# Eight terms of a depthwise convolution, for two of four channel tiles, as diagonal products on TensorE

## The reference, cut to what matters

```python
def conformer(glu):
    val, gate = jnp.split(glu, 2, axis=-1)
    y = depthwise_conv(val * jax.nn.sigmoid(gate), dw_conv) + dw_bias
    return jax.nn.silu(layer_norm(y, cln_g, cln_b))

def merge(o, z, glu):
    o = rms_norm(o, out_norm) * jax.nn.silu(z)
    return jnp.concatenate([o.reshape(B, L, GDN_WIDTH), conformer(glu)], axis=-1) @ w_out
```

## Time and profile before

| | |
|---|---|
| median of 3 runs | 2729.27 us |
| the profiled execution | 2721.98 us, span 2720.2 us, mean granted TensorE clock 0.978 |
| TensorE busy | 2588.2 us (95%) |
| VectorE busy | 1694.9 us (62%) |
| ScalarE busy | 1219.2 us (45%) |
| GpSimd busy | 667.3 us (25%) |
| the levels of the even mixer | 617.8 to 745.3 us of the span |
| all taps (L2684) | 120, the first at 510.0, the last at 756.9 us |

### The profile page before, as it was taken

How to read it: one execution, slowest core, us unless ns; L and a number is a source line. 1 busy time by engine, 2 the same in 40 slices (tenths; PEclk the granted TensorE clock), 3 DMA queues, 4 the chain that set the end, 5 groups by cost and what they waited for, 6 DMA issues and landing times.

```text
span 2720.2 us, 43296 instructions
## 1 busy us (share of the span) xinstructions
PE 2588.2 (95%) x16792; PEld 2235.0 (82%) x16792; DVE 1694.9 (62%) x3011; ACT 1219.2 (45%) x2304; POOL 667.3 (25%) x604
## 2 busy tenths in 40 slices
PE   8999999997879999999999998999989999999998
PEld 5778887886767888787888886789988888989888
DVE  5775465898777665455654445565564567746666
ACT  4223324751254432324333224656555568555674
POOL 1101112003203111022111112121125543655335
PEclk9999999998989999999999998999999999999999
DMA  6554441220003443432442441235544443444434
GB/s 262 171 178 144 163 147 63 78 85 2 3 1 109 163 160 137 154 122 87 165 163 102 171 141 63 99 120 185 183 144 147 140 147 125 165 146 142 146 125 140
DMA packets 115868, 352.78 MB, mean 130 GB/s; under 512 B 12752, under 2 KB 14928, under 8 KB 115280
## 3 DMA queue, kind: packets, MB, share of 16 engines
q1 hardware_dynamic: 115664, 350.01, 37.8%
HBM read 348.91 MB, written 1.05 MB: 129 GB/s over the span
## 4 chain that ended last, share of the span: by engine, by line
PE 79%; DVE 8%; ACT 6%; issue 3%; DMA 2%; POOL 2%; SPq 1%; DVEq 0%; ACTq 0%; POOLq 0%
PE ps L1886 21%; PE ps L1889 21%; PE ps L1887 21%; DMA ring<-w_stream 2%; ACT spl L2221 1%; PE ps L1951 1%; PE ps L1928 1%; DVE big L2684 1%; DVE spl L2467 1%; PE ps L2138 1%; PE ps L1960 1%; PE ps L1966 1%; PE ps L1898 1%; ACT big L2407 1%; PE ps L1900 1%
## 5 line engine op out<-in xcount | busy, mean ns | idle before, releaser
L1886 PE MATMUL ps<-bigr,spl 128*128 128x256 f32 (+1 forms) x3880 | 1323.7, 341 | 36.2 <-DVE spl L2467 13.9
L1889 PE MATMUL ps<-bigr,spl 128*128 128x256 f32 (+1 forms) x3880 | 1303.1, 336 | 5.5 <-POOL bigr L2947 5.3
L1887 PE MATMUL ps<-bigr,spl 128*128 128x256 f32 (+1 forms) x3880 | 1300.3, 335 | 0.0
L2467 DVE TENSOR_TENSOR spl<-ring,spl 128x512 fp32r<-128x512 f32 x840 | 662.5, 795 | 660.3 <-ACT spl L2221 656.4
L2221 ACT ACTIVATE spl<-ring 128x512 fp32r<-128x512 f32 x1024 | 632.9, 627 | 806.9 <-PE ps L1889 607.8
L1886 PEld LDWEIGHTS ps<-bigr,spl 128*128 128x128 f32 x3880 | 739.9, 191 | 132.3 <-issue 28.7
L1889 PEld LDWEIGHTS ps<-bigr,spl 128*128 128x128 f32 x3880 | 739.5, 191 | 87.5 <-POOL bigr L2947 11.8
L1887 PEld LDWEIGHTS ps<-bigr,spl 128*128 128x128 f32 x3880 | 740.3, 191 | 73.8 <-issue 1.7
L2947 POOL TENSOR_TENSOR bigr<-work,bigr 128x512 fp32r<-128x512 f32 (+1 forms) x200 | 210.4, 1056 | 947.6 <-ACT bigr L2225 947.6
L2942 POOL TENSOR_TENSOR spl<-ring,spl 128x512 fp32r<-128x512 f32 x184 | 249.5, 1357 | 284.0 <-ACT spl L2221 283.4
L2225 ACT ACTIVATE bigr<-work 128x512 fp32r<-128x512 f32 (+2 forms) x240 | 123.4, 517 | 272.1 <-DVE work L2552 166.6
(11 more groups left out here) (309 smaller groups left out, 2424.1 us busy)
## 6 DMA issues: line engine op xcount, KB each, us to landing
ring<-w_stream SPq DMA_DIRECT2D x512, 512.0 KB, 3.3
big<-w_stream SPq DMA_DIRECT2D x256, 256.0 KB, 3.2
big<-w_stream SPq DMA_DIRECT2D x16, 512.0 KB, 11.2
X<-x_t SPq DMA_DIRECT2D x2, 1024.0 KB, 13.8
cst<-consts SPq DMA_DIRECT2D x1, 1537.5 KB, 6.7
X<-mem_t SPq DMA_DIRECT2D x1, 1024.0 KB, 5.8
out_t<-X SPq DMA_DIRECT2D x8, 128.0 KB, 2.2
prm<-params SPq DMA_DIRECT2D x1, 252.5 KB, 2.8
```

The costliest lines, as they stand in the source:

```text
L1886: pe.matmul(out, hi, x[0], start=k == 0, stop=False)
L1887: pe.matmul(out, lo, x[0], start=False, stop=False)
L1889: finish(pe.matmul(out, hi, x[1], start=False, stop=k == nk - 1), tile, key if k == nk - 1 else None)
L2467: dve.tensor_tensor(lo_half(h), raw_half(h), hi_half(h), SUB).then_inc(*sig("lo", h, by="lo_dve"))
```

## The change

For tiles 2 and 3 VectorE does taps 0 to 22. Taps 23 to 30 become eight products on TensorE, added up in one PSUM bank per tile: the weights are a diagonal 128x128 matrix that holds the tap's value per channel, the moving operand is the shifted tile. ScalarE makes the diagonals, four at a time, from the identity, into a scratch tile of `sqs` (512 wide). A last VectorE instruction per tile, `conformer_join`, adds the bank to `CF[m]`.

A second generator, `diagonals`, deals this work: for tile 2, then tile 3, twice (one step of four diagonals, then four steps of one product each). It is advanced by one step in each of the 20 levels, right behind the two `level_p` and ahead of the side work; what is left runs after the levels. A tile's bank is held from its first step to its join. `cstep` now stops with the join of tile 2; the join of tile 3 is dealt in the scan.

```diff
-            def conformer(scan_taps):
+            def conformer(scan_taps, sums_):
                 for p in (0, 2):
-                    for j in range(31):
-                        if p and j == 29:
-                            scan_taps.append(True)
+                    for j in range(23 if p else 31):
                         for m in (p, p + 1):
                             yield "conformer", j, m
                             yield CUT
+                scan_taps.append(True)
+                for m in (2, 3):
+                    bank, bi = sums_[m]
+                    yield "conformer_join", m, bank
+                    banks.give(bi, ("conformer", 30, m))
+                    yield CUT
+
+            def diagonals(sums_):
+                for m in (2, 3):
+                    bank, free, bi = banks.get()
+                    for j0 in (23, 27):
+                        sq, sfree, i = sqs.get()
+                        yield "diagonal", m, j0, sq, sfree
+                        yield CUT
+                        for j in range(j0, j0 + 4):
+                            yield "diagonal_tap", m, j, sq[:, 128 * (j - j0):128 * (j - j0) + 128], bank, free
+                            yield CUT
+                        sqs.give(i, ("cf_pe", m, j0 + 3))
+                    sums_[m] = bank, bi
...
                             yield "level_p", h, d, lv, b, free
                             banks.give(bi, ("lvp", h, d, lv))
+                        yield from advance(dgen)
                         yield from advance(side)
                         yield from cstep()
...
                 seen = set()
+                for s in dgen:
+                    if s is not CUT:
+                        yield s
                 while not scan_taps:
                     yield from cstep()
...
+            def diagonal_tap(m, j, d, bank, free):
+                if j == 23:
+                    w.all(free, done)
+                    w.wait_ge(*done("glu_y", m))
+                w.wait_ge(*done("cf_diag", m, 23 if j < 27 else 27))
+                pe.matmul(two(bank), d, YP[m][:, :, j:j + 256], start=j == 23, stop=j == 30).then_inc(*sig("cf_pe", m, j))
...
+            def diagonal(m, j0, sq, free):
+                w.wait_ge(*done("cst"))
+                w.all(free, done)
+                for i in range(4):
+                    j = 31 * m + j0 + i
+                    ins = act.activation(sq[:, 128 * i:128 * i + 128], P("ident"), ACTF.Copy, scale=P("dwc", j, j + 1))
+                ins.then_inc(*sig("cf_diag", m, j0))
...
+            def conformer_join(m, bank):
+                w.wait_ge(*done("conformer", 22, m))
+                w.wait_ge(*done("cf_pe", m, 30))
+                dve.tensor_tensor(CF[m], CF[m], bank, ADD).then_inc(*sig("conformer", 30, m))
```

More of the change, by code:

```diff
@@ L939, in even_mixer @@
                 scan_taps = []
-                cgen, padded = conformer(scan_taps), set()
+                sums_ = {}
+                cgen, padded, dgen = conformer(scan_taps, sums_), set(), diagonals(sums_)
                 def cstep(n=1, scan=False):
@@ L2203, in tensor_program @@
                 tables, linear, by_token, ada, ada_raw, fill, fill_turn, ada_turn, ada_sum, colsum, spread, gate_columns, tail_columns, turn_kv,
-                gram, gate_rows, unit_turn, q_decay, level_p, level_u, u_values, w_keys, scan_v, scan_s, scan_own, head_turn,
+                gram, gate_rows, unit_turn, q_decay, level_p, level_u, u_values, w_keys, scan_v, scan_s, scan_own, diagonal_tap, head_turn,
                 scores, probs_turn, values, rope, index_weights, index_turn, index_heads)})
@@ L2429, in scalar_program @@
                 gates_in, gates_exp, gates_ratio, short_conv, conv_silu, conv_glu, z_silu, tail_columns, turn_kv, decay, unit_turn, q_decay,
-                u_values, w_keys, tail_keys, scan_out, head_squares, conformer_silu, head_root, head_gain, head_unit, softmax, probs_turn, gated, index_heads)})
+                u_values, w_keys, tail_keys, scan_out, head_squares, diagonal, conformer_silu, head_root, head_gain, head_unit, softmax, probs_turn, gated, index_heads)})
         def vector_program(dve, w):
@@ L2928, in vector_program @@
                 ln_mod, alpha_cols, ln_out, gates_in, gates_exp, gates_ratio, gates_series0, gates_series1, gates_series2, gates_scan, gates_back,
-                gates_rest, short_conv, qk_unit, conv_glu, conformer, gate_columns, tail_columns, decay, decayed, unit,
+                gates_rest, short_conv, qk_unit, conv_glu, conformer, conformer_join, gate_columns, tail_columns, decay, decayed, unit,
                 level_p, level_u, scale_u, scan_v, scan_s, scan_out, scan_own, conformer_norm, head_sums, head_inverse, head_scale, head_out, mem_unit, mem_scale, head_unit, scores, softmax,
```

## The result

Both kernels were timed in turns on the same chips, 20 executions of each. The changed kernel took 2730.51 us in the median (2725.43 to 2734.51), the kernel before 2726.58 us (2722.96 to 2729.49). The ratio is 1.0014, 95% interval 1.0008 to 1.0020: **3.9 us slower**, resolved from zero but under the 0.2% that the prediction named as its edge. So what came is its "same" (0.41) and not its "slower by over 0.2%" (0.47). It forecast +5.5 us, 2734.8 us on the median of three executions. Those three are among the 20, whose median is 2.7 us lower, so the forecast's distance to the measured time is 4.3 us, of which 1.6 us are the change and the rest is the base.

What follows compares the result with a forecast made beforehand. TensorE's chain was taken to bound most levels. Products on the path +11.6, VectorE's relief -5.5 and head 0's clock -0.6 gave +5.5 us, 2734.8 us on the median; range 2727.5 to 2740.5 for 8 in 10.

Steps and rivals of the forecast that it cites:

- rival A: Levels: VectorE bounds them and TensorE's products vanish in its waits; 2723.8 us, or 2718 with all twelve taps; chance 0.11.
- all eleven places: One in head 0, six in heads 1 and 2, four in head 3: products on the chain, together +11.6 us.
- the other five: Levels 4, 8, 32 of head 0 and level 16 of heads 1 and 2: products covered by waits, 0 us.
- 1.05 us for a product: Plain fp32 product on TensorE's chain, priced from the `q_decay` row: 1.05 us; from below 0.52, from above 2.1.
- VectorE gives back 5.5 us: Relief on the chain: tap at 708.82 -0.66, head 2's level 32 -2.6, head 3's clock -1.7, scan -0.5; together -5.5 us.
- Fills, joins and banks at zero: Levels and scan: fills in ScalarE's idle time, joins priced as replaced taps, bank waits held at 0, bound 0.6 a head.
- The stand of 2.62 us in head 3: Level 2 of head 3: TensorE's stand goes and its clock then holds at 2.4 GHz, -1.7 us.
- Head 0's clock at -0.6, heads 1 and 2's at nothing: Head 0's level 4 product shortens the stand, clock gain counted half, -0.6 (0 to -1.2); heads 1, 2 no gain.
- Rival B: Products keep TensorE's clock up, worth up to 6.2 us in heads 0 to 2; +1.1, 2730.5 us; chance 0.24.
- The scan at -0.5 and the rest at nothing: Scan: one of two vanishing taps was on the chain, -0.5 us; no term was given for what follows.
- The sum: Whole kernel: 11.6 - 5.5 - 0.6 = +5.5 us, 2734.8 us on the median.
- Its own marks: Wrong if product on path costs under 0.6 us, head 1 does not grow, heads 0-2's clock changes by over one stretch.

## Why the prediction was right or wrong

- **TensorE bounds most levels, not VectorE** (rival A's 0.11): right. Products are on the chain at all eleven places and at none of the other five. Without twelve taps the kernel gains 7.1 us, not 11, and with no tap gone but six moved it still gains 3.5, where A has 0.
- **1.05 us for a product**: right as to size, 1.06 at eight of the places and 0.87 at the three in front of `q_decay`; head 3's levels paid 1.11. That three of the eleven cost 0.87 makes the sum 0.5 us smaller.
- **VectorE gives back 5.5 us**: near, with two terms off. By the chain, level 32 of head 2 gave back 2.6 and the tap 0.7, as foreseen. But level 16 of head 2, put at nothing, gave back 0.6: with no tap of VectorE beside them, the second of each pair of GpSimd's products takes 0.73 us instead of 1.05 to 1.07. The first of the two, in the chain before and in that of the changed kernel:

```profile
712.03 1.05 POOL arow L2979
```

```profile
714.87 0.73 POOL arow L3023
```

  And in the scan the -0.5 did not come: where a tap of 0.52 us was on the chain there is now a join of 0.69.
- **Fills, joins and banks at zero**: nothing contradicts them. The stretch in front of `w_keys`, where the banks might have made TensorE wait, has the product at 662.30 us and `w_keys` right behind it at 663.36.
- **The stand of 2.62 us in head 3 goes, and the half clock behind it**: right. TensorE's `level_u` of level 2 comes at 724.02 us, 0.5 us after the last piece of `level_p`, and head 3 runs at a granted 1.00. From that `level_u` to `level_p` of level 4 the chain takes 3.9 us instead of 5.5: -1.6, where 1.7 was forecast.
- **Head 0's clock at -0.6, heads 1 and 2's at nothing**: this step failed. The stand in head 0 shrank from 2.65 to 1.59 us, as foreseen. The clock held behind it, and then in heads 1 and 2 as well. Rival B had listed these terms: 2.8 us in head 0 (0.6 of it in the forecast) and 1.7 in each of heads 1 and 2, 5.6 beyond the forecast. The chain gives them in one piece each. In head 0, from `level_u` of level 4 to GpSimd's first product it is 1.4 us shorter, and from `unit_turn` to the first `q_decay` 1.5 to 1.6; from `level_u` of level 2 to `level_p` of level 4 it is 1.6 us shorter in head 1 and 1.6 to 1.7 in head 2. That is 6.2 together, 5.6 beyond the forecast, as B has it. The end of the piece of head 1, `u_values` and `level_p`, before and changed (it starts at 655.85 and 657.43 us):

```profile
658.95 2.38 PE ps L2073 x32
661.33 0.93 PE ps L2049 x32
```

```profile
659.56 1.75 PE ps L2097 x32
661.31 0.99 PE ps L2073 x32
```

  Missing from the three heads against the forecast are 2.4, 1.7 and 2.4 us, 6.5 together: these 5.6, 0.6 from GpSimd and 0.5 from the cheaper products in front of `q_decay`, less some 0.2 of small pieces. What B had against itself, that the long stands at level 2 get no product, was the wrong test. These stands are still there in the timeline of the changed kernel, and the clock does not fall behind them. The rows are head 0's level 4, and level 2 of heads 1 and 2, where TensorE had stood 1.80 and 2.62 us:

```profile
633.89 0.34 PE L2085 MATMUL ps<-big 64*64 64x64 f32 x4 [1.59 <-DVE big L2766]
...
657.43 0.34 PE L2085 MATMUL ps<-work,arow 64*64 64x64 f32 x4 [1.79 <-DVE work L2766]
...
692.75 0.34 PE L2085 MATMUL ps<-big 64*64 64x64 f32 x4 [2.71 <-DVE big L2766]
```

- **The scan at -0.5 and the rest at nothing**: this failed the other way and hid part of the first miss. The scan grew by 1.8 us, with two taps fewer in it. The first group of 16 products of line L2094 (L2118 after) that the chain has behind the tap of 756.86 us, in the kernel before:

```profile
758.68 2.19 PE ps L2094 x16
```

  In the changed kernel the group at 758.29 us takes 3.78 us (in the chain above) and the next takes 2.19 again. From 758.0 to 765.0 us the granted clock is 0.65 in the changed kernel; in the 7 us from 755.0 before it is 0.95. The 1.6 us of this one group are most of the scan's 1.8. Six kernels have this longer scan at 0.79 to 0.83 (the changed one, the products alone, twice, the ten in stands, the taps moved, both together); without products it stays at 0.85, as it does with the ten idle ones. So part of the half clock came back later in five kernels that had got rid of it in the levels, and in one that had not (the taps moved). What decides this was not isolated.
- **The sum**: by its own terms the levels should have grown by 6 us; they shrank by half a microsecond. The total came near because +1.8 and +2.5 lay where the prediction had -0.5 and 0. The forecast's time lay in its range and its sign was right, but that is in good part luck: its balance of terms was B's in the levels, and what cancelled the miss stood in none of its rivals.
- **Its own marks**: it called itself wrong if the clock in heads 0 to 2 changed by more than one stretch. It did. Head 1 took 35.3 us, not 37.0.

So the change costs time because of where the products lie and not because TensorE does them: sixteen dealt one per level, eleven of them behind `level_p` on the chain, +3.9 us; ten of them mostly in TensorE's stands, -7.1. That all sixteen could be hidden so was not shown, as no run tried it.

## What to carry to other kernels

Before work is moved to the engine that carries the chain, list that engine's stands and who ends them, and deal the new work into those. One per level is regular, and it put 11 of 16 pieces on the path. Where the granted clock is below 1 in a stage, price the whole stage's half clock as a term with two ends and not as a remark: here it was as large as the relief of VectorE (6.2 us in heads 0 to 2 against 5.5). And cut the time into stages in two or more profiles of each kernel, since a total that agrees can be the sum of two misses.

## What the runs showed of the hardware that was not expected

TensorE's clock fell to 1.2 GHz behind stands of 1.64 to 2.65 us in the kernel before, in stretches such as 725.0 to 728.4 us, and it stayed at 2.4 GHz behind stands of 1.59, 1.79 and 2.71 us in the changed kernel, whose TensorE was busy 112 us of the stage's 132 instead of 107. So one stand's length did not tell whether the clock would fall. Ten useless products made the kernel 4.4 us faster (0.9984). The falls came at nearly the same places of the stage when the same kernel was profiled again (levels at 0.87 and 0.87 before; 0.97, 0.99 and 0.97 after). They could also come elsewhere: emptying three slots of VectorE in two heads took the scan, where no instruction of TensorE changed, from 0.86 to 0.79.

GpSimd's fp32 product of two 128x256 tiles took 1.05 to 1.07 us beside a tap of VectorE and 0.73 without one.

A plain fp32 product of 128x128 by 128x512 costs 1.06 us alone, and 0.86 to 0.88 behind another of its form. A join from PSUM takes 0.68 us, no more than a tap from SBUF (0.74 in the median).
